# Feed-forward part of two layers on the unnormed x, with the norm's factor behind the second product

## The reference

```python
def rms_norm_2(x, w):
    y = xf * lax.rsqrt(jnp.mean(xf * xf, axis=-1, keepdims=True) + RMS_EPS)
    return (y * w.astype(jnp.float32)).astype(x.dtype)

for layer in range(2):
    ...                                         # mixers, then:
    x = x + mixed @ w_out[layer]
    h = rms_norm_2(x, mlp_norm_w[layer])
    x = x + jnp.square(jax.nn.relu(h @ w_up[layer])) @ w_down[layer]
return rms_norm_2(x, final_norm_w)
```

## Time and profile before

| | |
|---|---|
| median of 3 runs | 1387.16 us (1387.02 to 1387.91) |
| the profiled execution's own time | 1388.44 us |
| its span, first to last instruction | 1386.7 us |
| TensorE busy | 1366.0 us (99%) |
| VectorE / ScalarE busy | 652.7 us (47%) / 263.1 us (19%) |
| mean granted TensorE clock | 0.997 of full speed |
| share of the chain that ended last on TensorE | 96% |

### The profile page before, as it was taken

How to read it: one execution, slowest core, us unless ns; L and a number is a source line. 1 busy time by engine, 2 the same in 40 slices (tenths; PEclk the granted TensorE clock), 3 DMA queues, 4 the chain that set the end, 5 groups by cost and what they waited for, 6 DMA issues and landing times.

```text
span 1386.7 us, 21689 instructions
## 1 busy us (share of the span) xinstructions
PE 1366.0 (99%) x9136; PEld 1042.5 (75%) x9136; DVE 652.7 (47%) x1484; ACT 263.1 (19%) x561; POOL 7.2 (1%) x16
## 2 busy tenths in 40 slices
PE   8999999999999999999999999999999999999997
PEld 5888886454445444454488879999998878999997
DVE  2477463111111111111288837775446783777544
ACT  2234102000000000000243421220004352122000
POOL 0000000000000000000000000000000000000000
PEclk9999999999999999999999999999999999999999
DMA  9997756999999999999944234444444414444410
GB/s 393 359 416 283 268 206 248 417 422 420 421 421 421 421 420 421 420 421 421 421 166 155 86 122 160 175 167 168 173 161 152 153 62 151 154 165 170 172 72 32
DMA packets 51236, 362.53 MB, mean 261 GB/s; under 512 B 6065, under 2 KB 6385, under 8 KB 7873
## 3 DMA queue, kind: packets, MB, share of 16 engines
q1 hardware_dynamic: 48528, 353.39, 64.2%
q10 hardware_dynamic: 2032, 5.70, 1.4%
q0 software_dynamic: 576, 2.01, 0.4%
HBM read 357.92 MB, written 1.06 MB: 259 GB/s over the span
## 4 chain that ended last, share of the span: by engine, by line
PE 96%; DMA 2%; DVE 1%; issue 0%; ACT 0%; DVEq 0%; POOL 0%; POOLq 0%
PE bank L1112 26%; PE bank L857 23%; PE bank L550 20%; PE bank L562 5%; PE bank L845 4%; PE bank L868 4%; PE bank L1257 2%; PE bank L1048 2%; DMA ring<-in_weights 2%; PE bank L678 2%; PE bank L1161 1%; PE bank L1212 1%; PE bank L662 1%; PE bank L622 1%; PE bank L1238 1%; PE bank L1225 1%
## 5 line engine op out<-in xcount | busy, mean ns | idle before, releaser
L550 PE MATMUL bank<-h,ring 128*128 128x256 f32 x832 | 184.1, 381 | 0.1
L550 PEld LDWEIGHTS bank<-h,ring 128*128 128x128 f32 x832 | 156.9, 190 | 22.8 <-issue 1.7
L857 PE MATMUL bank<-ring,x_s 128*64 128x512 f32 x768 | 168.0, 592 | 2.5 <-DMA ring<-in_weights 1.5
L857 PEld LDWEIGHTS bank<-ring,x_s 128*64 128x64 f32 x768 | 56.1, 137 | 111.2 <-issue 111.2
L1112 PE MATMUL bank<-hid,ring 128*128 128x128 f32 x912 | 115.6, 275 | 0.0
L1112 PE MATMUL bank<-h,ring 128*128 128x128 f32 x896 | 113.8, 275 | 0.0
L1112 PEld LDWEIGHTS bank<-hid,ring 128*128 128x128 f32 x912 | 108.6, 192 | 0.0
L1112 PEld LDWEIGHTS bank<-h,ring 128*128 128x128 f32 x896 | 107.0, 192 | 0.1
L1979 DVE TENSOR_TENSOR act<-act,bank 128x512 f32<-128x512 f32 x16 | 11.0, 687 | 197.1 <-PE bank L857 197.1
L1112 PE MATMUL bank<-sq,ring 128*128 128x128 f32 x720 | 95.1, 275 | 0.0
L1112 PEld LDWEIGHTS bank<-sq,ring 128*128 128x128 f32 x720 | 87.6, 192 | 0.0
(11 more groups left out here) (359 smaller groups left out, 1679.3 us busy)
## 6 DMA issues: line engine op xcount, KB each, us to landing
ring<-in_weights SPq DMA_DIRECT2D x288, 1024.0 KB, 13.4
ringx<-in_weights SPq DMA_DIRECT2D x48, 1024.0 KB, 20.9
x<-in_x SPq DMA_DIRECT2D x1, 1024.0 KB, 5.1
pool_a<-in_cst ACTq DMA_DIRECT2D x1, 1024.0 KB, 6.5
bias<-bias_rows POOLq DMA_DIRECT2D x1, 1024.0 KB, 16.3
ring<-cq ACTq DMA_DIRECT2D x8, 128.0 KB, 2.4
ring<-ck ACTq DMA_DIRECT2D x8, 128.0 KB, 2.4
out<-h ACTq DMA_DIRECT2D x2, 512.0 KB, 2.9
```

The costliest lines, as they stand in the source:

```text
L550: ins = e.matmul(u.ap[:, 0:S], w[:, k * width + j * P:k * width + (j + 1) * P], acts[:, k, :], start=k == 0, stop=k == kc - 1)
L857: ins = e.matmul(g.bank[bank][ex * SLOTS:(ex + 1) * SLOTS, :], stat(m)[:, ex * SLOTS:(ex + 1) * SLOTS], pair[ex][:, m * 512:(m + 1) * 512] ...
```

## The change

- One tile of `w_up` is plain in place of two (`PLAIN = 1`), so 15 are sevens and 30 in all.
- The sevens of `w_up` read `xw` and not h; h is no longer computed in this part. The differences are those of `xw`, and t1 gets a place of its own (`t1_last`), since `xw` must stay whole.
- Neither the root nor rs2 is used here. `scr2` (r^2) multiplies the results of `w_down`: one instruction of 512 columns for each two chunks of the sevens, one of 256 columns for each chunk of the last plain tile (into `pair_a`), each ahead of the addition to x.
- Relu and square of the plain tile of `w_up` go to ScalarE.
- The squares of x lie in `g.h`. VectorE adds them behind the differences; the sums for sevens 0 and 1 are made between the parts of `lout`.
- TensorE's norm matmuls stand behind seven 1; VectorE's `dve_norm` stands behind seven 4 (and behind the sums for seven 6). The differences of the hidden blocks move to behind sevens 3, 7, 11 and 14.

```diff
+PLAIN = 1
+UPS = 16 - PLAIN
-UPS = 14
 ...
 def pe_norm_added(e, g, n):
-    sq = g.sq2 if n else g.sq
+    sq = {0: g.sq, 3: g.h, 5: g.h}.get(n, g.sq2)
 ...
 # pe_layer
-    for j in range(2):
-        w = g.filled(e, layer_tile(l, 16 + j))
-        for jj in range(2):
-            oc = 2 * j + jj
-            pe_chunk(e, g, ("up", l, oc), w, jj, 256, KC, g.xw, raw(1))
-            if oc == 0:
-                pe_norm_added(e, g, n + 1)
-        g.owed += 1
+    w = g.filled(e, layer_tile(l, 16))
+    for jj in range(2):
+        pe_chunk(e, g, ("up", l, jj), w, jj, 256, KC, g.xw, raw(1))
+    g.owed += 1
     for i in range(SEVENS):
         pe_seven(e, g, l, i)
+        if i == 1:
+            pe_norm_added(e, g, n + 1)
 ...
 # pe_seven
-    (b11, t1), (b21, b22) = token_quarters(g.h if i < UPS else g.hid[:, 8 * b:8 * b + 8, :])
+    (b11, t1), (b21, b22) = token_quarters(g.xw if i < UPS else g.hid[:, 8 * b:8 * b + 8, :])
-    if i >= UPS and b == 3:
+    if i < UPS or b == 3:
         t1 = g.t1_last
 ...
 # act_layer
-        e.activation(g.sq2[:, 2 * j:2 * j + 2, :], g.x[:, 2 * j:2 * j + 2, :], ACT.Square).then_inc(s["squares"], 1)
-    act_root(e, g, 3 + 2 * l, g.rs2, g.scr2)
+        e.activation(g.h[:, 2 * j:2 * j + 2, :], g.x[:, 2 * j:2 * j + 2, :], ACT.Square).then_inc(s["squares"], 1)
+    for jj in range(2):
+        ps = g.full(e, "up", l, jj)[:, 0:S]
+        g.read(("up", l, jj), e.activation(g.hid[:, jj, :], ps, ACT.Relu))
+        g.evac(e, "up", l, jj)
+    e.activation(g.hid[:, 0:2, :], g.hid[:, 0:2, :], ACT.Square).then_inc(s["hid_ready"], 1)
 ...
 # dve_layer, for j in range(4) of lout
-        if j > 1:
-            dve_add_squares(e, g, n + 1, j - 1, 2)
-    dve_add_squares(e, g, n + 1, 3, 2)
-    dve_weight_sums(e, g, l, 0)
-    dve_norm(e, g, n + 1, None, g.h, g.rs2, g.scr2)
-    dve_rs_scaled(e, g, n + 1)
-    e.wait_ge(s["h_scaled"], KC * (n + 2))
-    dve_differences(e, g, g.h, g.h_diff)
-    ... (the four plain chunks times rs2, relu, square)
-    dve_weight_sums(e, g, l, 1)
+        if 1 <= j <= 2:
+            dve_weight_sums(e, g, l, j - 1)
+    e.wait_ge(s["xw"], KC * (2 * l + 2))
+    dve_differences(e, g, g.xw, g.h_diff, g.t1_last)
+    for j in range(1, 4):
+        dve_add_squares(e, g, n + 1, j, 2, g.h)
     for i in range(SEVENS):
 ...
             dve_seven(e, g, key, (UPS + 4) * l + UPS + mp + 1, g.pair_c)
             g.evac(e, *key, 1)
             two = g.x[:, 2 * mp:2 * mp + 2, :].rearrange("p c t -> p (c t)")
+            e.wait_ge(s["recip"], RECIPS[n + 1])
+            both = g.pair_c.rearrange("p (c t) -> p c t", c=2)
+            g.after(e)
+            step.up(e.tensor_tensor(both, both, g.scr2.unsqueeze(1).to_broadcast([P, 2, S]), ALU.mult))
+            g.after(e)
             ins = e.tensor_tensor(two, two, g.pair_c, ALU.add)
 ...
         if i + 2 < SEVENS:
             dve_weight_sums(e, g, l, i + 2)
-        if i in (2, 6, 10, 13):
+        if i == 4:
+            dve_norm(e, g, n + 1, None, g.h, g.rs2, g.scr2)
+        if i in (3, 7, 11, 14):
             done = i // 4
-            if done == 0:
-                e.wait_ge(step.sem, chunks_done)
-            e.wait_ge(s["hid_ready"], UPS * l + 4 * done + 2)
+            e.wait_ge(s["hid_ready"], 16 * l + 4 * done + 4)
             dve_differences(...)
     for jj in range(2):
-        g.read(("down", l, jj), e.tensor_tensor(g.x[:, k, :], g.x[:, k, :], ps[:, 0:S], ALU.add))
+        g.read(("down", l, jj), e.tensor_tensor(g.pair_a, ps[:, 0:S], g.scr2, ALU.mult))
         g.evac(e, "down", l, jj)
+        e.tensor_tensor(g.x[:, k, :], g.x[:, k, :], g.pair_a, ALU.add).then_inc(s["x_down"], 1)
+        e.wait_ge(s["x_down"], 5 * l + 4 + jj)
```

More of the change, by code:

```diff
@@ L502 @@
 RECIPS = {0: 1, 1: 2, 2: 4, 3: 5, 4: 6, 5: 7, 6: 8}
-ROOTS = {0: 1, 1: 2, 2: 4, 3: 6, 4: 7, 5: 9, 6: 10}
+ROOTS = {0: 1, 1: 2, 2: 4, 4: 6}
 ADDED = {0: 1, 1: 2, 3: 3, 4: 4, 5: 5, 6: 6}
 def pe_norm_added(e, g, n):
-    sq = g.sq2 if n else g.sq
+    sq = {0: g.sq, 3: g.h, 5: g.h}.get(n, g.sq2)
     u = g.take(e, ("ss", n))
@@ L541, in h_ready @@
 def h_ready(e, g, n, k):
-    e.wait_ge(g.s["h_shifted" if n < 2 else "h_scaled"], KC * n + k + 1)
+    e.wait_ge(g.s["h_shifted" if n < 2 else "h_scaled"], KC * (n if n < 2 else 1 + n // 2) + k + 1)
 def pe_chunk(e, g, key, w, j, width, kc, acts, ready, bank=None):
@@ L1053, in pe_layer @@
         g.owed += 1
-    for j in range(2):
-        w = g.filled(e, layer_tile(l, 16 + j))
-        for jj in range(2):
-            oc = 2 * j + jj
-            pe_chunk(e, g, ("up", l, oc), w, jj, 256, KC, g.xw, raw(1))
-            if oc == 0:
-                pe_norm_added(e, g, n + 1)
-        g.owed += 1
+    w = g.filled(e, layer_tile(l, 16))
+    for jj in range(2):
+        pe_chunk(e, g, ("up", l, jj), w, jj, 256, KC, g.xw, raw(1))
+    g.owed += 1
     for i in range(SEVENS):
         pe_seven(e, g, l, i)
-    w = g.filled(e, layer_tile(l, 18 + SEVENS))
-    e.wait_ge(s["hid_ready"], UPS * (l + 1))
+        if i == 1:
+            pe_norm_added(e, g, n + 1)
+    w = g.filled(e, layer_tile(l, 16 + PLAIN + SEVENS))
+    e.wait_ge(s["hid_ready"], 16 * (l + 1))
     for jj in range(2):
@@ L1096, in pe_seven @@
     key, b, of = seven_block(l, i)
-    w = g.filled(e, layer_tile(l, 18 + i))
+    w = g.filled(e, layer_tile(l, 16 + PLAIN + i))
     (a11, a12), (a21, a22) = quarters(w)
     s1, s2, s3, s4 = (g.sums[i % 2][:, n * 512:(n + 1) * 512].rearrange("p (k c) -> p k c", k=4) for n in range(4))
-    (b11, t1), (b21, b22) = token_quarters(g.h if i < UPS else g.hid[:, 8 * b:8 * b + 8, :])
+    (b11, t1), (b21, b22) = token_quarters(g.xw if i < UPS else g.hid[:, 8 * b:8 * b + 8, :])
     t2, t3, t4 = g.h_diff if i < UPS else g.hid_diff[b]
-    if i >= UPS and b == 3:
+    if i < UPS or b == 3:
         t1 = g.t1_last
@@ L1514, in act_layer @@
         g.evac(e, "lout", l, j)
-        e.activation(g.sq2[:, 2 * j:2 * j + 2, :], g.x[:, 2 * j:2 * j + 2, :], ACT.Square).then_inc(s["squares"], 1)
-    act_root(e, g, 3 + 2 * l, g.rs2, g.scr2)
+        e.activation(g.h[:, 2 * j:2 * j + 2, :], g.x[:, 2 * j:2 * j + 2, :], ACT.Square).then_inc(s["squares"], 1)
[4 more added lines that the diff above has]
+    e.activation(g.hid[:, 0:2, :], g.hid[:, 0:2, :], ACT.Square).then_inc(s["hid_ready"], 1)
     for i in range(UPS):
-        two = g.hid[:, 4 + 2 * i:6 + 2 * i, :]
+        two = g.hid[:, 2 + 2 * i:4 + 2 * i, :]
         act_first_product(e, g, ("up7", l, i))
@@ L1535, in act_down @@
         act_first_product(e, g, ("down7", l, k // 2))
[L1536 to L1539, removed]
+    e.wait_ge(g.s["x_down"], 5 * l + (k // 2 if k < 6 else k - 3) + 1)
 def act_turn_halves(e, g, l, which):
@@ L2125, in dve_layer @@
     dve_layer_prob(e, g, l, 1)
-    e.wait_ge(s["root"], 5 + 3 * l)
+    e.wait_ge(s["root"], 5 + 2 * l)
     e.tensor_tensor(o, o, inv, ALU.mult).then_inc(s["o_scaled"], 1)
@@ L2168, in dve_layer @@
         if i < UPS:
-            dve_seven(e, g, key, (UPS + 4) * l + i + 1, g.hid[:, 4 + 2 * i:6 + 2 * i, :].rearrange("p c t -> p (c t)"))
+            dve_seven(e, g, key, (UPS + 4) * l + i + 1, g.hid[:, 2 + 2 * i:4 + 2 * i, :].rearrange("p c t -> p (c t)"))
         elif b == of - 1:
@@ L2181, in dve_layer @@
             ins.then_inc(s["x_down"], 1)
-            e.wait_ge(s["x_down"], 3 * l + mp + 1)
+            e.wait_ge(s["x_down"], 5 * l + mp + 1)
             for oc in (2 * mp, 2 * mp + 1):
```

## The result

| | median | runs | ratio to before (95%) |
|---|---|---|---|
| before | 1387.43 us | 4 | |
| changed | 1401.72 us (1400.49 to 1402.64) | 4 | 1.0106 [1.0093, 1.0118] |

The account below looks back on a forecast made before the run. The prediction took TensorE's list and any wait entering it as the bound. It summed -1.30 (tiles) + 9.14 (bank stops) + 0.46 (last instruction) to +8.3 us, so 1387.2 + 8.3 = 1395.5 us, range 1393.5 to 1400.5.

Parts of the forecast that it names:

- One tile changes its way: TensorE, one `w_up` tile a layer goes from plain to seven: 0.65 us less, 1.30 us for two layers.
- VectorE's list ahead of the first seven: VectorE between `lout` and seven 0: differences ready 2.0 us before the plain tile ends, cost 0.
- The banks: TensorE stops at seven 5 until VectorE reads `ss` from bank 6: 4.57 us a layer, 9.14 us in all.
- The stated upper end: Upper bound of the stop at seven 5: 5.0 us a layer, if hand-over and first matmul's start cost some tenths.
- The factor behind the second product: VectorE's extra multiplication after `w_down`: hidden in the groups and at layer 0's end, +0.46 us at layer 1's end.
- The root's table: ScalarE's square-root table load behind the last square, for the final norm: cost 0, with 0.9 us to spare.
- the first rival: Same stops at seven 5, but TensorE's clock falls in them: middle 1397.8 us, chance 0.36.
- the stops at full clock: The forecast case: TensorE stops at seven 5 in both layers without a clock fall, 1395.5 us, chance 0.48.
- the 3.1 a fall: Bound on TensorE's extra time for one climb back of the clock: up to 3.1 us, likely half of that.
- the case with one fall: First rival with the clock falling in one of the stops: 1397 to 1398.6 us.
- the worst of two falls: First rival with the clock falling in both stops: up to 1401.7 us, left out of the range.

Follow-up runs that it names:

- experiment 7: Changed kernel with VectorE's norm read behind seven 2 and the last hidden block scaled ahead, behind seven 27: 1385.66 us, ratio 0.9989.
- experiments 1 and 2: Changed kernel with, behind seven 2, VectorE's norm read in the one and TensorE's norm matmuls in the other: 1385.55 and 1385.11 us.
- experiment 1: Changed kernel with VectorE's norm read behind seven 2 in place of seven 4: 1385.55 us, ratio 0.999.
- experiment 4: Changed kernel with 10 unread matmuls put into seven 5 before it takes its second bank: 1394.90 us, ratio 1.0054.

## Why the prediction was wrong, step by step

**One tile changes its way:** right. 12.51 / 2 = 6.25 us for a seven, 6.91 for the plain tile; -1.30 us in the stretch of experiment 7 to the hundredth.

**VectorE's list ahead of the first seven:** right. VectorE's work on the last part of `lout` starts 0.70 us behind TensorE's end of it (0.68 by the prediction, 1174.78 - 1174.10), and the differences end at 1182.8 against an end of the plain tile at 1184.8: 2.0 us to spare, as worked out. VectorE's timeline there, against the earlier trace rows (this trace lies 3.8 us later):

```profile
1178.59 0.68 DVE L2143 TENSOR_TENSOR x<-x,bank 128x512 f32<-128x512 f32 x1
1179.30 0.62 DVE L2146 TENSOR_SCALAR hm<-x,prm 128x256 f32<-128x256 f32 x2
...
1182.13 0.69 DVE L2230 TENSOR_TENSOR sq<-hm,sq 128x512 f32<-128x512 f32 x1
1182.74 2.28 DVE L2058 TENSOR_TENSOR h<-h 128x512 f32<-128x512 f32 x3
```

**The banks:** the mechanism was right, place, number and releaser, and experiments 1 and 2 show it. The size was a little small. VectorE's list came out as worked out from the earlier trace rows: `dve_seven` 4 at E(4) + 0.15 (1217.08), the read at 1221.05, done at 1221.47. What was missing is TensorE's start behind it: 0.25 us of issue, not 0.04, and another 0.24 until the chain is up to speed. 4.57 us a layer were 4.80 + 0.24 = 5.04, 0.47 more. The stated upper end was 5.0, which had allowed for some tenths at this place.

**The factor behind the second product:** right. It is hidden in the groups of sevens (no break in the pieces of 175.09 us in experiment 1) and costs 0.46 us at the end, where there are now two links, L2193 and L2195, where the earlier trace rows had L2200:

```profile
1388.08 0.43 DVE hal L2193
1388.51 0.02 issue
1388.54 0.43 DVE x L2195
```

**The root's table:** right. The load stands behind the last square, and the root waits 1.00 us more, for VectorE and not for a drain:

```profile
1389.43 1.28 ACT L1617 ACT_TABLE_LOAD   x1
1391.71 0.31 ACT L1617 ACTIVATE rs<-scr 128x128 f32<-128x128 f32 x1 [1.00 <-DVE scr L2364]
```

The Trainium skill's switch of 2.66 us (ScalarE: Activation LUTs, What ACT_TABLE_LOAD costs) is again not borne out: the root starts 1391.71 - 1389.43 = 2.28 us after the load began, although it also waited for VectorE.

**The step that failed is the choice between the forecast and the first rival.** The prediction gave "the stops at full clock, 0.48" and entered the clock with 0 in the sum, on the word that "the single fall that the trace shows doesn't say that it always comes that soon". In these stops it came that soon every time. In the three traces with stops of 4.3 and 4.8 us the clock fell in all six, between 2.0 and 4.0 us after the last matmul (the trace of before had shown 3.8).

The reading behind that word was wrong too: the clock was not at 1.00 until 1382.5 us in the trace of before, and the fall at its end was not its only one. It was at 0.50 behind 225.4 us as well, after waits of 1.20 and 0.74 us, much shorter than the stops that were forecast.

The price of a fall: in five of the six stops the clock was low for 6.8 us, in one for 3.4, and what of this lay behind the end of the stop was worked at half speed: 4.0 and 5.9 us in the first trace of the changed kernel, half of which are 2.0 and 3.0; the rows give 2.16 - 0.24 = 1.9 and 3.07 - 0.24 = 2.8. Both lie under the 3.1 a fall that the prediction had as its bound from the earlier trace rows, but the half of it that it thought likely, 1.5, was low. That the bound held is in part luck: the profile gives the clock as 1.00 in TensorE's first stretch, so no row shows that the 3.1 us there were the clock's. The sum with the falls in it would have been 8.3 + 2 x 0.47 (stop and start) + 1.9 + 2.8 (clock) = 13.9. Even as a rival it stood too low, at 1397.8, since this is the middle of the case with one fall, and the range ended at 1400.5, since it left out the worst of two falls.

The rule of the Trainium skill (TensorE: Matmul & The Clock Gate, HAM oscillation), told in the prediction as speaking for this rival, held in all six stops of 4.3 and 4.8 us; in the four of 2.3 us and the two of 0.8 us the clock stayed up.

## What to carry to other kernels

Where banks go round in a circle, a result that is read late must be counted forward to the instruction that takes its bank next: one place more or one less in that count was worth 15 us here, with no difference in work. At an engine that is otherwise never idle, price a stop by its length, plus the restart, plus the work done at the lower clock behind it; a stop of over 4 us cost half as much again as it lasted. Give the clock a term of its own in the sum when a stop of about the length behind which the trace shows a fall is forecast, and look through the whole trace for such falls: here the clock fell in six of six stops over 4 us, in none of six of 2.3 us and less, and yet in seven of twelve traces behind two short waits at 225 us. So the length of one wait doesn't tell it alone.

## What the runs showed of the hardware

- A stop of TensorE costs 0.24 us more than it lasts, at 0.8 us as at 2.3 (1400 records in 156.57 us against 156.33), and its hand-over from VectorE takes 0.25 us, where the one from ScalarE to two short matmuls at the end takes 0.04. When the array had been kept busy up to 0.3 us before, the hand-over from VectorE was 0.04 too, as the chain of experiment 4 shows:

```profile
872.79 0.04 issue
872.84 0.38 PE bank L1115
```

- Useless matmuls paid: filling the two stops made the kernel 6.8 us faster by the medians and 5.1 by the stretch, though the first useful matmul behind a stop starts only 0.2 us sooner.
- The clock came back after 6.8 us in five of the six stops in which it fell and after 3.4 us in one, and TensorE's records behind the stops took 1.4 to 2.9 us longer for it (157.97 to 159.45 us against 156.57).
- The clock can fall behind short waits, and in some executions only: at 225 us in seven of twelve traces, behind waits of 1.20 and 0.74 us, at 1.4 to 2.8 us a time.
